# The last attention of a two-block transformer on one Trainium2 core: another order of scores, exponentials and output units

## What is computed

```python
q = qg[..., :N_HEADS * Dh].reshape(...) * (Dh ** -0.5)
gates = sigmoid(qg[..., N_HEADS * Dh:])          # 3 per head
p_c = masked_softmax(q @ k_cmp + bias, mask_c)   # 15 compressed keys
p_s = masked_softmax(q @ k_sel + bias, mask_s)   # selected keys
p_w = masked_softmax(q @ k_win + bias, mask_w)   # window keys
o = g0 * (p_c @ v_cmp) + g1 * (p_s @ v_sel) + g2 * (p_w @ v_win)
out = o @ w_o
```

## Time and profile before

| what | value |
|---|---|
| median of three runs | 1522.26 us (1521.37 to 1522.62) |
| profiled execution, its time | 1522.35 us |
| its span in the profile | 1520.5 us |
| mean granted TensorE clock | 0.985 |
| busy share of the span: PE, PEld, DVE, ACT, POOL | 97%, 88%, 61%, 43%, 6% |
| share of DMA engine time, queue of the weights | 50.0% |
| the last attention, first scores to `down_last` | 1223.54 to 1311.49 us |

### The profile page before, as it was taken

How to read it: one execution, slowest core, us unless ns; L and a number is a source line. 1 busy time by engine, 2 the same in 40 slices (tenths; PEclk the granted TensorE clock), 3 DMA queues, 4 the chain that set the end, 5 groups by cost and what they waited for, 6 DMA issues and landing times.

```text
span 1520.5 us, 25321 instructions
## 1 busy us (share of the span) xinstructions
PE 1469.3 (97%) x10475; PEld 1341.2 (88%) x10484; DVE 929.7 (61%) x1363; ACT 659.0 (43%) x834; POOL 95.8 (6%) x78
## 2 busy tenths in 40 slices
PE   8998998999999999999999999999999998999997
PEld 6988987899899999999789999999999876799996
DVE  5877357555665555657875555646555647765556
ACT  5655534333433334545244334425333448543332
POOL 0012141000020000100020000100000100100000
PEclk9999998999999999999999999999999999999999
DMA  7443344776577555655355555667555430465551
GB/s 257 145 137 100 137 140 153 218 216 218 179 239 259 194 190 183 197 182 191 115 199 189 190 182 185 202 199 234 194 191 182 156 113 29 139 205 185 192 193 56
DMA packets 191526, 268.43 MB, mean 177 GB/s; under 512 B 5740, under 2 KB 164752, under 8 KB 191182
## 3 DMA queue, kind: packets, MB, share of 16 engines
q1 hardware_dynamic: 186336, 250.05, 50.0%
q0 software_dynamic: 4224, 15.91, 3.1%
q10 hardware_dynamic: 878, 1.21, 0.3%
HBM read 261.92 MB, written 4.19 MB: 175 GB/s over the span
## 4 chain that ended last, share of the span: by engine, by line
PE 84%; DVE 9%; ACT 3%; DMA 2%; issue 1%; POOL 0%; DVEq 0%; ACTq 0%
PE bank L730 82%; PE bank L753 2%; DVE split L1981 2%; DMA ring<-in_ffn_w 2%; ACT split L1510 1%; DVE resid L2058 1%; DVE resid L2066 1%; DVE stats L2037 1%; DVE resid L2035 1%; DVE arena L2530 1%; ACT act_out L1532 0%; DVE arena L2573 0%; DVE stats L1995 0%; DVE arena L2178 0%; ACT gain_rows L1636 0%
## 5 line engine op out<-in xcount | busy, mean ns | idle before, releaser
L730 PE MATMUL bank<-hT_hi,split 128*128 128x256 f32 (+1 forms) x3984 | 720.5, 281 | 7.5 <-ACT act_out L1648 5.4
L1981 DVE TENSOR_TENSOR split<-ring,split 128x2048 fp32r<-128x2048 f32 x212 | 484.2, 2286 | 375.2 <-ACT split L1510 369.9
L730 PEld LDWEIGHTS bank<-hT_hi,split 128*128 128x128 f32 (+1 forms) x3984 | 617.4, 189 | 17.0 <-issue 10.8
L1510 ACT ACTIVATE split<-ring 128x2048 fp32r<-128x2048 f32 (+1 forms) x224 | 426.9, 1907 | 360.0 <-PE bank L730 321.4
L730 PE MATMUL bank<-hT_lo,split 128*128 128x256 f32 (+1 forms) x1992 | 559.1, 281 | 0.0
L730 PEld LDWEIGHTS bank<-hT_lo,split 128*128 128x128 f32 (+1 forms) x1992 | 377.1, 189 | 2.3
L730 PE MATMUL bank<-split,hid_hi 128*128 128x512 f32 x992 | 288.7, 397 | 0.0
L730 PEld LDWEIGHTS bank<-split,hid_hi 128*128 128x128 f32 x992 | 182.6, 188 | 40.8 <-issue 0.8
L730 PE MATMUL bank<-split,hT_hi 128*128 128x256 f32 (+1 forms) x896 | 179.1, 298 | 7.2 <-DVE split L1981 4.4
L730 PE MATMUL bank<-split,hid_lo 128*128 128x512 f32 x496 | 159.6, 395 | 0.0
L730 PEld LDWEIGHTS bank<-split,hT_hi 128*128 128x128 f32 x896 | 143.5, 190 | 15.9 <-issue 5.7
(11 more groups left out here) (212 smaller groups left out, 965.5 us busy)
## 6 DMA issues: line engine op xcount, KB each, us to landing
ring<-in_ffn_w SPq DMA_DIRECT2D x132, 1024.0 KB, 5.1
ring<-in_w_in SPq DMA_DIRECT2D x19, 1024.0 KB, 5.2
ring<-in_w_mlp_in SPq DMA_DIRECT2D x16, 1024.0 KB, 6.3
ring<-in_w_mlp_out SPq DMA_DIRECT2D x16, 1024.0 KB, 5.0
ring<-in_sgu_w_in SPq DMA_DIRECT2D x16, 1024.0 KB, 5.4
ring<-in_sgu_w_out SPq DMA_DIRECT2D x8, 1024.0 KB, 4.8
ring<-in_kv_w SPq DMA_DIRECT2D x6, 1024.0 KB, 5.4
ring<-in_w_out SPq DMA_DIRECT2D x4, 1024.0 KB, 4.9
```

The source lines that it names most:

```text
L730: ins = pe.matmul(o, lhsT, rhs, start=start, stop=stop)
L1510: act.activation(halves(q, n)[0], ring[:, u % SLOTS, 0:n], ACT.Copy).then_inc(hi_ready, 1)
L1981: dve.tensor_tensor(lo, ring[:, u % SLOTS, 0:n], hi.bitcast(F32), ALU.subtract).then_inc(split_ready, 1)
```

## The change

A fourth place for probabilities, the normalised rows `xn_flat` (they hold the bias of batches 0 to 3 until then), and a table of places; PE scores three batches ahead; DVE normalises ahead of the maxima; output units move. In full but for the places where only `prob[m]` became `prob[pair_place(i)]`:

```diff
-PROBS = 3
+PROBS = 4
@@ plan_tiles
-        elif name[0] == "ov" and name[1] < N_PAIR - 2:
+        elif name[0] == "ov" and name[1] < N_PAIR - 3:
             bank = 7
@@
-        prob = [cx_all..., k_cmp..., prob_late]
+        prob = [cx_all..., k_cmp..., prob_late,
+                xn_flat.rearrange("p (k s) -> p k s", k=8)]
@@
+        def pair_place(i):
+            return (0, 1, 2, 0, 3, 1, 2, 0)[i]
+        def pair_held(i):
+            return {3: 0, 5: 1, 6: 2, 7: 3}.get(i)
@@ PE
+            def down_half(unit, act, b):
+                for k in range(2):
+                    for w, a, _, _ in passes(k, 1):
+                        for h in range(2):
+                            ins = mm(acc[b * 2 + h][:, :], act(a, k)[:, b * P:(b + 1) * P],
+                                     unit[w][:, k, h * 512:(h + 1) * 512], False, False)
+                            settle(ins)
+                return ins
@@ PE
             queries(4)
+            pair_scores(1)
             compressed_scores(0)
-            pair_scores(1)
             queries(5)
             pair_probs(0)
             queries(6)
@@
             pair_values(0)
             queries(7)
+            pair_scores(3)
             compressed_scores(1)
-            for i in range(1, N_PAIR - 2):
+            for i in range(1, N_PAIR - 3):
                 pair_probs(i)
-                pair_scores(i + 2)
+                pair_scores(i + 3)
                 pair_values(i)
                 if i == 2:
                     compressed_probs(1)
-            pair_probs(N_PAIR - 2)
+            pair_probs(N_PAIR - 3)
             pe.wait_ge(score_taken, 4 * N_PAIR)
-            tile_copied(pe, ("ov", N_PAIR - 3))
+            tile_copied(pe, ("ov", N_PAIR - 4))
             clear_acc()
             down_split(*wo(0))
+            pair_values(N_PAIR - 3)
+            pair_probs(N_PAIR - 2)
+            unit, rows = wo(1)
+            down_half(unit, rows, 0)
             pair_values(N_PAIR - 2)
             pair_probs(N_PAIR - 1)
-            down_split(*wo(1))
+            down_half(unit, rows, 1).then_inc(unit_used, 1)
             pair_values(N_PAIR - 1)
             down_last(wo(2), lambda: wo(3), 8)
@@ ACT
             queries(4)
+            pair_exps(1)
+            queries(5)
             compressed_exps(0)
-            queries(5)
             pair_probs(0)
-            pair_exps(1)
+            round_unit(("wo", 0))
             queries(6)
             compressed_probs(0)
             pair_exps(2)
-            round_unit(("wo", 0))
             queries(7)
             round_attended(0)
             for i in range(1, N_PAIR):
@@
-                elif i == N_PAIR - 2:
-                    round_unit(("wo", 1))
-                    round_unit(("wo", 2))
-                else:
-                    round_unit(("wo", 3))
+                if i >= N_PAIR - 3:
+                    if i == N_PAIR - 1:
+                        act.wait_ge(scored, 4 * N_PAIR)
+                    round_unit(("wo", i - N_PAIR + 4))
@@ DVE, pair_maxima
-                if i >= PROBS:
-                    dve.wait_ge(tile_done, TILES[("pt", i - PROBS, 3)][2] + 1)
+                if pair_held(i) is not None:
+                    dve.wait_ge(tile_done, TILES[("pt", pair_held(i), 3)][2] + 1)
@@ DVE
+            pair_maxima(1)
+            pair_normalize(0)
             compressed_maxima(0)
-            pair_normalize(0)
-            pair_maxima(1)
             compressed_weights(0)
+            pair_normalize(1)
             pair_maxima(2)
-            pair_normalize(1)
             low_unit(("wo", 0))
+            pair_maxima(3)
             dve.wait_ge(rel_back[1], 16)
             compressed_maxima(1)
             low_attended(0)
             for i in range(1, N_PAIR):
-                if i + 2 < N_PAIR:
-                    pair_maxima(i + 2)
                 if i + 1 < N_PAIR:
                     pair_normalize(i + 1)
+                if i + 3 < N_PAIR:
+                    pair_maxima(i + 3)
                 if i == 1:
                     compressed_weights(1)
-                if i == N_PAIR - 2:
-                    low_unit(("wo", 1))
-                    low_unit(("wo", 2))
-                elif i == N_PAIR - 1:
-                    low_unit(("wo", 3))
+                if i >= N_PAIR - 3:
+                    if i == N_PAIR - 1:
+                        dve.wait_ge(tile_done, TILES[("pt", N_PAIR - 2, 3)][2] + 1)
+                    low_unit(("wo", i - N_PAIR + 4))
                 if i < N_PAIR - 1:
                     low_attended(i)
```

More of the change, by code:

```diff
@@ L425, in two_blocks @@
         cx = cx_all.rearrange("p (s j g i) -> p s j g i", s=2, j=16, g=NG)
-        prob = [cx_all.rearrange("p (k s) -> p k s", k=8), k_cmp.rearrange("p a b c s -> p (a b c) s"), prob_late]
+        prob = [cx_all.rearrange("p (k s) -> p k s", k=8), k_cmp.rearrange("p a b c s -> p (a b c) s"), prob_late,
+                xn_flat.rearrange("p (k s) -> p k s", k=8)]
         hidc = take(at, 2, 2, NG, 32)
@@ L794, in branch @@
                 return ins
+            def down_half(unit, act, b):
[6 more added lines that the diff above has]
+                return ins
             def down_split(unit, act):
                 for b in range(NB):
[L800 to L805, removed]
+                    ins = down_half(unit, act, b)
                 ins.then_inc(unit_used, 1)
@@ L1415, in pair_probs @@
                             ins = turn(o[:, (br * 2 + k) * P:(br * 2 + k + 1) * P],
-                                       prob[i % PROBS][:, 2 * p + br, k * P:(k + 1) * P])
+                                       prob[pair_place(i)][:, 2 * p + br, k * P:(k + 1) * P])
                             settle(ins)
@@ L1871, in pair_exps @@
                     for k in (2 * p, 2 * p + 1):
-                        s = prob[m][:, k, 0:P * (p // 2 + 1)]
+                        s = prob[pair_place(i)][:, k, 0:P * (p // 2 + 1)]
                         ins = act.activation(s, s, ACT.Exp, bias=neg_max[:, m, k:k + 1], scale=-1.0,
@@ L2529, in pair_maxima @@
                         k = 2 * p + br
-                        ins = dve.tensor_tensor_reduce(prob[m][:, k, 0:w], pair_bank(i, p)[:, br * S:br * S + w],
+                        ins = dve.tensor_tensor_reduce(prob[pair_place(i)][:, k, 0:w], pair_bank(i, p)[:, br * S:br * S + w],
                                                        rel[h // 8][:, h % 8, S - w:S], -1.0, -GONE, ALU.add, ALU.min,
@@ L2571, in pair_normalize @@
                 for k in range(8):
-                    s = prob[m][:, k, 0:P * (k // 4 + 1)]
+                    s = prob[pair_place(i)][:, k, 0:P * (k // 4 + 1)]
                     ins = dve.tensor_scalar(s, s, row_rcp[:, m, k:k + 1], None, ALU.mult)
```

## The result

The changed kernel takes 1534.95 us (median of six runs, 1531.73 to 1536.11), the kernel before 1521.82 (six runs, 1517.3 to 1523.6). The ratio is 1.0086, interval 1.0068 to 1.0103: **slower by 13.1 us**, where 3.6 us less were forecast. The sign was wrong, and the time lies outside the range. The profiled execution took 1536.11 us, with a span of 1534.3, 13.8 longer than before; its mean granted clock, 0.985, is the old one.

A forecast was written before the change was run, and what follows sets the result against it. PE, busy 97% of the span, was taken as the bound, so only its waits or low clock could be won. From the profiled 1522.35 us, -5.1 at full clock gave 1517.3, plus 1.4 for one fall 1518.7; range 1516.6 to 1522.0.

The forecast's parts named there:

- PE's instructions stay the same, so I write PE's new list with the lengths of the rows: Last attention: PE's new times are built from start-to-start lengths in the old trace, adding waits where PE must stand.
- the one on the slow side: Rival "Slower": every loop turn falls to the low clock for a long stretch, 4 * 2.65 = 10.6 us; 1527.9; chance 0.05.
- First batches: Start of the last attention: scores 4 start 24.8 us behind scores 1, with added waits costed at nothing.
- 3.2 + 2.2: Behind the old compressed scores: 3.2 us of PE waiting and 2.2 us of low clock go.
- Loop: Attention turns: 6.90 us instead of 6.63, four instead of five; PE stands 2.4, 1.8, 1.1 and 1.6 us.
- V + 3.96: Loop: score tile 3 starts 3.96 us after V, the end of values i - 1 on PE.
- Output units: Last early transposes' end to `down_last`: 20.6 us instead of 17.31, adding values 5 and one transpose set; other waits cost nothing.
- The sum at full clock: All terms without clock falls: `down_last` at 1306.4 instead of 1311.49, -5.1 us, giving 1517.3 us.
- one fall: The clock falls once, behind the loop's first stand, costing 1.4 us: the forecast, 1518.7; chance 0.40.
- The change does what it is written for: Rival: DVE isn't late in the loop, stands of 6.9 us shrink to some 2; 1512.4; chance 0.05.
- Each turn falls: Rival: every loop turn falls with short low stretches, adding 5.6 us; 1522.9, no change; chance 0.06.
- Two or three falls: Rival: the clock also falls in loop turns 2 and 4; 1520.1 to 1521.5; chance 0.22.

The follow-up runs named there:

- e1_room_for_four: The kernel before with only the six small softmax tables at four places instead of three, order unchanged: 1539.8 us against 1521.46, ratio 1.0124.
- e3_split_moved: The kernel before with 192 unused bytes straight ahead of `split`, tables and order unchanged: 1539.65 us, ratio 1.0121.
- e2_same_addresses: The changed kernel with three of the six tables at two places, so large tensors lie where they did before: 1516.0 us, ratio 0.9971 against before.
- e9_first_batches_only: The kernel before, old loop and addresses, with only the first batches in the new order: 1515.72 us against 1522.0, ratio 0.996.
- e4_low_half_later: `e2_same_addresses` with DVE taking the low half of batch i - 1 behind the normalising of i + 1 in early turns: 1515.61 us, ratio 0.9968 against before.

## Why the prediction was wrong, and where it was right

**The step that failed** is the one ahead of the sum: "PE's instructions stay the same, so I write PE's new list with the lengths of the rows". The instructions did stay the same; their spacing did not. The six tables that `PROBS = 4` makes longer stand nowhere in the sum: their bytes were put at nothing, without a reason, and all lengths outside the last attention were taken as given. `e1_room_for_four` puts the missing term at +18.3 us, more than three times the gain, and `e3_split_moved` at +18.2 for `split` alone. What the runs show in place of unchanged lengths is a spacing of 120.0 ns instead of 116.7 in 5976 matmuls, because `split` lies 192 bytes further from `hT_hi`. No rival held it: the one on the slow side (1527.9, falls of the clock) would have missed as well.

**The order.** Without the addresses the forecast stands: -3.6 us against the median; measured -5.5 in `e2_same_addresses` by the medians, and -4.4 (-2.6 to -6.4) by its ratio.

- *First batches.* Scores 4 were put 24.8 us behind scores 1. In `e2_same_addresses` they came 26.2 behind, 1.3 of it because the transposes ahead ran at the half clock. `e9_first_batches_only` shows that this part alone gives as much as the whole order, as the terms of the sum have it: 3.2 + 2.2 won there, some 6.5 won against 6.9 lost in the loop.
- *Loop.* At full clock right to 0.01 us: turn 6.90, score tile 3 at V + 3.96. The stands were 0.80, 1.60, 0.53 and 1.35, where 2.4, 1.8, 1.1 and 1.6 were forecast. Each is some 0.2 short because the transposes take 1.46 and not 1.25; PE is there later, and DVE sets the turn all the same. The rest of the first and the third is PE coming late at the half clock. In `e4_low_half_later`, where it did not, the first two are 2.46 and 1.71. The turn of the changed order is longer than the old one, as forecast, and the loop's part of the change is worth nothing: the old loop with the new first batches is as fast.
- *Output units.* From the last transposes of the loop to `down_last`: forecast 1.25 + 20.6 = 21.85, measured 22.41 (1322.25 - 1299.84). PE waited for no low half of a unit.
- *The sum at full clock*, -5.1, gives 82.85 us from the first scores to `down_last`. `e9_first_batches_only`, which has no fall, took 83.05 by another way through the loop. `e2_same_addresses` took 84.73, with two falls: 0.1 for the first, 1.3 for the second (below), and 0.5 more in the output units.

**The clock.** I expected one fall, behind the first stand; the changed kernel has three, `e2_same_addresses` two, `e4_low_half_later` one, `e9_first_batches_only` none. Two places were not foreseen: 1249.4 to 1252.6, in the dense first batches, behind a wait of 0.31 us, and 1269.8 to 1273.1, in the transposes ahead of the first stand, behind a wait of 0.28 at 1266.85. What a fall costs depends on what runs in it. In `e2_same_addresses` the first (1256.7 to 1260.1) only fills the stand behind it: score tile 3 of the first turn comes 28.48 us behind scores 1, forecast 28.39. The second lies on the values, which end 4.22 us behind their score tile 3 (1268.80 to 1273.02), against 2.94 at full clock (1283.86 to 1286.80): 1.3 us. I took 1.4 for one fall. That two falls came to the same 1.4 is luck.

The Trainium skill, "TensorE: Matmul & The Clock Gate", section "HAM oscillation — how this bites in real kernels", describes a loop whose clock falls in every turn, at a wait of some 3 to 5 us in each. The stands here are shorter, and their length alone doesn't decide: one of 1.60 (1281.84) and one of 1.71 (1264.06 in `e4_low_half_later`) were followed by a fall, one of 1.35 (1296.90) and one of 2.46 (1256.81 in `e4_low_half_later`) were not. What makes the difference these runs leave open.

**The rivals.** "The change does what it is written for" (1512.4) is out: DVE was late, by the amounts forecast. "Each turn falls" is out too. "Two or three falls" is what happened inside the stretch, and it was not what set the result.

## What to carry to other kernels

A constant that sizes a table moves every buffer behind it. Ahead of judging an order, build the new order at the old addresses and the old order at the new ones, two kernels that separate the terms; and in the two traces, compare first when the first changed instruction starts. If it starts late already, the cause is not in the order, and a row with the same busy share and another count in the same window says that PE itself runs at another pace. Where PE sets the time, try some distances between the two operands of its matmuls and keep the best by measurement: 96 bytes of padding were worth some 21 us here (by the ratios, 0.9825 / 0.996 = 0.986), the best order 6.3.

## What was not expected of the hardware

- The spacing of back-to-back 128x256 matmuls at full clock depends on how far the two operands lie apart in the partition, within 256 bytes: 119.9 ns at 0, 118.3 at 32, 113.6 at 64, 117.6 at 96, 120.0 at 160, 116.7 at 224. No kernel put `hT_hi` and `split` at 128 or 192. At 64 one stretch ran at 117.8, so another cause takes part, and the mechanism stays open. The Trainium skill, "TensorE: Matmul & The Clock Gate", section "Back-to-back issue gap", says that weight load and matmul together set the spacing, and gives figures by the number of columns alone; these runs show a change of over 5% (113.6 to 120.0) with the columns kept.
- Neither the busy share nor the length of a matmul shows it: 100% in both kernels from 1095 to 1195, 0.28 us in both rows, and 700 against 718 matmuls.
- The clock fell behind waits of no more than 0.31 us (1249.4 and 1269.8 in the changed kernel), and not behind one of 2.46 (1256.81 in `e4_low_half_later`).
